# Recurrent mixer: the convolution's first tap on ScalarE instead of VectorE

## The reference

```
def recurrent_mixer(x, w_in, conv_w, conv_b, gate_a_w, gate_a_b, gate_x_w, gate_x_b, lam, w_out):
    y, r = jnp.split(x @ w_in, 2, axis=-1)
    y = jax.nn.gelu(y)
    r = causal_depthwise_conv(r, conv_w, conv_b)   # out = b + xp[t]*w[0] + xp[t+1]*w[1] + xp[t+2]*w[2] + xp[t+3]*w[3]
    h = rg_lru(r, gate_a_w, gate_a_b, gate_x_w, gate_x_b, lam)
    return (y * h) @ w_out
```

## Time and profile before

| | |
|---|---|
| time, median of 3 runs (lowest to highest) | 1524.43 us (1524.0 to 1524.75) |
| the profiled execution: its time / its span from first to last instruction | 1525.94 us / 1524.0 us |
| mean clock granted to PE in it | 0.994 of full speed |
| busy share of the span: PE, DVE, ACT, POOL | 97%, 69%, 50%, 21% |
| DVE first tap (L1678) | 8 instructions, 4.1 us busy |
| DVE taps two to four (L1680) | 24 instructions, 11.5 us busy |
| load of one unit of `rec_w_in`, issue to landing (median) | 3.7 us |
| where the recurrent stage lies in the span | about 208 to 277 us |

### The profile page before, as it was taken

The page is one execution under the profiler, slowest core; times in us unless marked ns, Lnnn a source line. Parts: engine busy times, 40 slices in busy tenths (PEclk is TensorE's granted clock), DMA queues, the critical chain, the costliest instruction groups (busy, mean ns, idle before and its releaser), DMA issues.

```text
span 1524.0 us, 31453 instructions
## 1 busy us (share of the span) xinstructions
PE 1480.7 (97%) x11939; PEld 1460.6 (96%) x11939; DVE 1052.0 (69%) x1999; ACT 765.5 (50%) x1270; POOL 318.6 (21%) x392
## 2 busy tenths in 40 slices
PE   7999998999999999999999999999999999999998
PEld 7999998899999999999999999889999999899898
DVE  6666578766655666557766656888678778876883
ACT  5454448555444554445554545446644453565442
POOL 4111113211101111014321114453320125231000
PEclk9999999999999999999999999999999999999999
DMA  6656754465555655554565555533343554334333
GB/s 207 186 179 200 241 166 139 152 189 184 181 174 185 186 184 181 173 188 154 162 192 180 179 176 157 152 107 116 91 119 107 164 145 123 99 98 125 111 117 120
DMA packets 245275, 239.65 MB, mean 157 GB/s; under 512 B 15160, under 2 KB 244392, under 8 KB 245048
## 3 DMA queue, kind: packets, MB, share of 16 engines
q1 hardware_dynamic: 245176, 238.29, 50.9%
HBM read 237.21 MB, written 1.05 MB: 156 GB/s over the span
## 4 chain that ended last, share of the span: by engine, by line
PE 84%; DVE 10%; ACT 2%; issue 2%; POOL 1%; DMA 0%; SPq 0%; DVEq 0%; ACTq 0%; POOLq 0%
PE bank L552 25%; PE bank L554 25%; PE bank L553 25%; DVE w_lo L1523 3%; PE bank L878 1%; PE bank L818 1%; PE bank L836 1%; ACT w_hi L967 1%; PE bank L801 1%; DVE work L1563 1%; DVE work L1680 1%; PE bank L884 1%; PE bank L894 1%; PE bank L817 1%; PE bank L837 0%
## 5 line engine op out<-in xcount | busy, mean ns | idle before, releaser
L1523 DVE TENSOR_TENSOR w_lo<-raw,w_hi 128x1024 fp32r<-128x1024 f32 (+1 forms) x456 | 563.0, 1244 | 303.8 <-ACT w_hi L967 303.5
L552 PE MATMUL bank<-x_hi,w_hi 128*128 128x256 f32 (+1 forms) x2480 | 719.0, 290 | 2.2 <-DVE w_lo L1523 2.2
L554 PE MATMUL bank<-x_hi,w_lo 128*128 128x256 f32 (+1 forms) x2480 | 707.1, 285 | 0.0
L553 PE MATMUL bank<-x_lo,w_hi 128*128 128x256 f32 (+1 forms) x2480 | 706.2, 285 | 0.0
L967 ACT CAST w_hi<-raw 128x1024 fp32r<-128x1024 f32 (+1 forms) x456 | 464.9, 1030 | 261.2 <-PE bank L554 250.1
L552 PEld LDWEIGHTS bank<-x_hi,w_hi 128*128 128x128 f32 x2480 | 476.0, 192 | 4.1 <-issue 2.0
L553 PEld LDWEIGHTS bank<-x_lo,w_hi 128*128 128x128 f32 x2480 | 476.1, 192 | 1.0
L554 PEld LDWEIGHTS bank<-x_hi,w_lo 128*128 128x128 f32 x2480 | 475.6, 192 | 0.0
L552 PE MATMUL bank<-y_hi,w_hi 128*128 128x256 f32 (+1 forms) x1088 | 310.2, 285 | 8.0 <-DVE y_lo L1534 8.0
L554 PE MATMUL bank<-y_hi,w_lo 128*128 128x256 f32 (+1 forms) x1088 | 309.5, 284 | 0.0
L553 PE MATMUL bank<-y_lo,w_hi 128*128 128x256 f32 (+1 forms) x1088 | 309.4, 284 | 0.0
(11 more groups left out here) (288 smaller groups left out, 1248.8 us busy)
## 6 DMA issues: line engine op xcount, KB each, us to landing
raw<-in_ffn_w_in_dram SPq DMA_DIRECT2D x176, 512.0 KB, 3.6
raw<-in_w_in_dram SPq DMA_DIRECT2D x100, 512.0 KB, 3.6
raw<-in_ffn_w_out_dram SPq DMA_DIRECT2D x64, 512.0 KB, 4.2
raw<-in_w_out_dram SPq DMA_DIRECT2D x32, 512.0 KB, 3.5
raw<-in_ffn_w_out_dram SPq DMA_DIRECT2D x32, 384.0 KB, 3.0
raw<-in_rec_w_in_dram SPq DMA_DIRECT2D x16, 512.0 KB, 3.7
raw<-in_sg_w_in_dram SPq DMA_DIRECT2D x16, 512.0 KB, 3.4
raw<-in_rec_w_out_dram SPq DMA_DIRECT2D x8, 512.0 KB, 3.4
```

What stands on the lines that cost most here:

```text
L552: mm(acc, wh, xh, start=first and j == 0, stop=False)
L553: mm(acc, wh, xl, start=False, stop=False)
L554: i_ = mm(acc, wl, xh, start=False, stop=last and j == n - 1)
L1523: TT(w_lo[:, s, 0:n, :], raw[:, s, 0:n, :], w_hi[:, s, 0:n, :].bitcast(fp32), SUB).then_inc(lo_made, 1)
```

## The change

The first tap with the bias, `w[0]*x + b`, is computed by ACT as an activation (Identity with a scale and a bias for each channel). A new function `taps0(p)` does it for the two tiles of pair p, each as soon as `tile_read` says that DVE has written it. It stands in ACT's loop at the second step of pairs 0 to 3 (r = 1, 3, 5, 7), behind the cast of that step and behind the root at r = 1, and ahead of `gates(range(4))` at r = 5 and of `decays(range(4))` at r = 7. DVE's `conv1` loses tap 0, and its tap 1 waits for the new semaphore `conv_tap0`, tile by tile. Taps 1 to 3 stay where they were.

```
@@ act:
+            def taps0(p):
+
+                for c in (2 * p, 2 * p + 1):
+                    act.wait_ge(tile_read, 2 * pb + c + 1)
+                    activation(rec_x[:, c, :], rec_p[:, c, 0:SEQ], ACT.Identity, scale=pcol("rec_conv_w", c),
+                               bias=pcol("rec_conv_b", c)).then_inc(conv_tap0, 1)
...
                     split_w(U + LEAD)
                     if r == 1:
                         root(1, META)
+                    if r in (1, 3, 5, 7):
+                        taps0(r // 2)
                     if r == 5:
                         gates(range(4))
@@ dve:
             def conv1(p):
 
-                for k in range(4):
+                for k in range(1, 4):
                     for c in (2 * p, 2 * p + 1):
                         src, w = rec_p[:, c, k:k + SEQ], pcol("rec_conv_w", k * NC8 + c)
-                        if k == 0:
-                            i_ = TS(rec_x[:, c, :], src, w, pcol("rec_conv_b", c), MUL, ADD)
-                        else:
-                            i_ = STT(out=rec_x[:, c, :], in0=src, scalar=w, in1=rec_x[:, c, :], op0=MUL, op1=ADD)
+                        if k == 1:
+                            dve.wait_ge(conv_tap0, c + 1)
+                        i_ = STT(out=rec_x[:, c, :], in0=src, scalar=w, in1=rec_x[:, c, :], op0=MUL, op1=ADD)
                         if k == 3:
                             i_.then_inc(conv_new, 1)
```

More of the change, by code:

```diff
@@ L339, in build_stack @@
             sem(n) for n in ("conv_new", "gates_mm", "gates_sig", "gated_in", "ax_new", "a2_new", "mult2", "mult_new"))
-        rec_gelu, rec_bx, scanned = sem("rec_gelu"), sem("rec_bx"), sem("scanned")
+        rec_gelu, rec_bx, scanned, conv_tap0 = sem("rec_gelu"), sem("rec_bx"), sem("scanned"), sem("conv_tap0")
         sg_gelu, sg_sqs, sg_sum, sg_rms = sem("sg_gelu"), sem("sg_sqs"), sem("sg_sum"), sem("sg_rms")
```

## The result

The changed kernel takes 1529.72 us in the median of its eight executions, against 1524.7 us of the kernel before, run beside it. One of the eight took 2044.63 us at a mean granted clock of 0.652 and is left out from here on; the other seven lie between 1527.53 and 1532.55 us, with a median of 1528.39. The ratio of the times is 1.0026 with a 95% interval of 1.0014 to 1.0037, about 4 us more (2.1 to 5.6). The profiled execution is the fastest of the seven: 1527.53 us, span 1525.7 us, 1.7 us longer than the span before. So the loss was forecast, and its size (3.2 us) lies inside the interval; but the pair of profiles shows less and the ratio somewhat more. Both have to be explained.

The account below looks back on a forecast made before the run. PE, busy 97% of the span, was taken to bound the kernel, waiting here for DVE and ACT's cast. DVE's savings counted nothing, the late cast +3.2 us: 1524.43 + 3.2 = 1527.6 us, range 1523.8 to 1529.8.

Parts of the forecast that it names:

- What bounds the kernel: PE is busy 97% and loses 8.3 us here; moving the cast at 252.71 moves the stage's end one for one.
- Part 1: DVE's conv rounds: without the first tap, but with the hand-over to ACT, DVE saves 0.40 us a pair.
- T: Start of a pair's evacuation by DVE: before the change 216.78, 223.25 and, for pair 3, 237.28 us.
- Part 2: ACT runs in order, so taps ahead of gates and tanh delay its casts; the one at 252.71 starts 3.22 us late.
- the five times: ACT's forecast starts: gates' table load 230.48, cast 234.69, tanh 239.49, casts 244.12 and 255.93 us.
- I count nothing: Pair 2's first tap overlapping POOL's work moves into DVE's wait for the cast, where it neither costs nor saves.
- an ACT that is in time: Rival: ACT hides its taps, so 1.6 to at most 2.2 us come off, 1522.2 to 1522.8; chance 0.12.
- Sum: DVE's savings come to nothing and ACT's late cast adds 3.2 us: span 1527.2, time 1527.6 us.
- 0.51 and 0.46: Chances forecast for the verdicts slower (0.51) and same (0.46), told apart at about 0.2%, 3.05 us.
- The upper bound of +4.7: Main case's loss in us if both pairs' taps on ACT are as slow as the slowest old tap, 831 ns.
- The clock: Rival: half clock behind PE's longer wait reaches the output product's next unit, up to +3.0 us more, 1530.6; chance 0.07.
- Table loads: Rival: Identity needs its own table, so ACT loads twice more, at r = 5 and 7, 1.28 us each: 1530.2; chance 0.04.

Follow-up runs that it names:

- wait_only: Kernel before, DVE computing all taps, with ACT only made to wait at r = 5 and 7 until that step's pair is evacuated: stage +2.35 us, ratio 1.0015.
- taps_01: The change for pairs 0 and 1 only, DVE computing the first taps of pairs 2 and 3: stage -0.37 us against the kernel before, ratio 1.0001.
- late_before: Kernel before with POOL's squares of the decay made to wait until all taps are done: stage -0.93 us, ratio 1.0007.
- inter_012: The change for pairs 0, 1 and 2 only, pair 2's taps placed amid the gates: stage -1.02 us against the kernel before, ratio 0.9997.
- late_01: taps_01 with POOL's squares of the decay made to wait until all taps are done: 1523.69 us against 1526.24 of the kernel before, ratio 0.9986.

## Why the prediction held, point by point

**What bounds the kernel.** Right. The cast that frees the tail moved by 3.20 us and the stage by 3.24, one for one. One reading was too low: a stop of PE costs more than the idle time in its row (2.65 us for the two waits of 2.18).

**Part 1, DVE's saving of 0.40 a pair.** Right as long as DVE is free of POOL: pair 1 is evacuated at 222.85, pair 2 at 228.93 (forecast 222.85 and 228.92). Taps 2 to 4 follow at T + 1.16, the tap takes 0.594.

**Part 2, ACT's late casts.** Right, with each of the five times within 0.03 us, and the idle times of DVE at 2.95 (forecast 3.0) and 3.24 (forecast 3). wait_only shows the cause without any tap: the wait costs 2.35 us by itself. That the other 0.9 are the taps and the table load behind them is an argument and not measured, since in wait_only DVE's taps also ran into POOL, which they don't in the change.

**"I count nothing" for POOL.** True of the change, since the taps of pairs 2 and 3 took 2.74 us there, free of POOL, and DVE waited afterwards anyway. But it hid a term. The rival of an ACT that is in time was priced at -1.6 to -2.2 us without it. taps_01, with two pairs the nearest thing to that rival, gained 0.37, and 0.74 more than late_before once the squares were out of the way. With three pairs inter_012 gained 1.02, too little for a verdict of faster (0.9997, 0.9988 to 1.0006). Priced by that run the rival was a gain of about 1 us, which the times don't show. The rows of the kernel before had the sign of it: pair 3's first tap at 1.10 us and its others at 3.30, beside POOL's squares.

**Sum.** 3.2 us forecast, 3.24 and 3.27 measured in the stage; the ratios, 1.0026 and 1.0018, are 4.0 and 2.7 us, on either side of it. Against 0.2% (3.05 us) one is above, one below, and the forecast had 0.51 and 0.46 for the two. The span was forecast at 1527.2 us and is 1525.7: the two profiled spans differ by only 1.7 us, since the half-clock stretches near 1261 and 1299 us fell worse in the one of before. That the total lands so near the stage's 3.2 is partly luck, with 0.9 to 1.5 us of half clock added behind the stage and nearly 3 us given back further on in the profile. The upper bound of +4.7 doesn't follow from its steps: a tap of 831 ns is 0.23 us over the 0.60 of the sum, four of them 0.92, which gives +4.1; 4.7 comes out only if the difference is taken from the 448 ns of DVE's tap. With taps of 0.594 us it didn't matter.

**The clock.** The forecast gave 0.07 to a low stretch that reaches into the output product. One does in both profiles of the change, for 0.9 and 1.5 us, but also in all eleven others that aren't of the kernel before. The forecast's step read a single execution of the kernel before as if it were the rule. How often the kernel before has such a stretch is open.

**Table loads.** Right: L1062 has no load on its line, and that at 230.50 is the gates'.

## What to carry to other kernels

Before work is moved to an engine with slack, look at what its program has queued behind the place: a wait there delays all of it, and an average of 50% busy says nothing of that. Moving a tap beside work that doesn't queue behind it (pairs 0 and 1) gained, moving the same tap ahead of the gates lost. Where a gain is smaller than forecast, look whether the engine now works beside another one that slows it, as DVE did beside POOL's squares. And when the cure is tried together with the change, run the cure alone too: more than half of late_01's gain was the cure's.

## What the runs showed of the hardware

VectorE beside GpSimd: two `tensor_scalar` of 128x256 in SBUF took 1.10 to 1.49 us instead of 0.74, and six `scalar_tensor_tensor` 3.07 to 4.40 us instead of 2.71, while GpSimd multiplied tiles in SBUF. GpSimd paid too: its four squares took 3.61 us in late_01 against 2.33 in the change, where VectorE waited for a cast meanwhile:

```profile
243.11 2.33 POOL L1432 TENSOR_TENSOR work<-work 128x256 f32<-128x256 f32 x4 [7.47 <-ACT work L1084]
```

The Trainium skill's "SBUF — State Buffer", "Who interferes with whom", has the port pair that the two share as an exclusive lock, so that one of them waits until the other's instruction is through; it names VectorE operations in a two-port mode, and those with two SBUF inputs while GpSimd reads SBUF. The rows agree in direction; they don't show which instruction waited for which.

TensorE behind a stop: the next matmuls come later by more than the idle time in the row, 0.84 us where the row has 0.62, and 1.81 where it has 1.56.

TensorE's clock: level 0.50 (1.2 GHz) was granted for some microseconds at places that differ between two executions of one program (mean 0.98 and 0.94 from 1250 to 1340 us). In late_01 it fell near 276 us behind waits of 1.33 and 0.53 us. Executions of the kernel before spread from 1523.1 to 1529.5 us by the runs beside these experiments, six microseconds where the effects studied are one to three.
